# Two transformer blocks on one core: a prologue with its stores and late loads moved behind the first group, one product for the bias lines, an early first slab and a last row in halves

## What is computed

```
mod = silu(c) @ w_ada + b_ada                       # 2048 -> 3 * 2048
shift, scale, gate = split(mod, 3)
h = rmsnorm(x, pre_g) * (1 + scale) + shift
q, k, v, gate_a, u, gate_p = split(h @ w_in)
y_a = windowed_gqa(q, k, v, rel_table, sink) * silu(gate_a)
y_p = multiscale_pool(u, w_pool_grp, pool_scale) * silu(gate_p)
g_a, g_p = split(sigmoid(h @ w_merge + b_merge))
o = (g_a * (y_a @ w_br_attn) + g_p * (y_p @ w_br_pool)) @ w_out
x = x + gate * rmsnorm(o, post_g)
```

## Time and profile before

| | us |
|---|---|
| median of 3 runs (lowest, highest) | 2450.28 (2445.57, 2456.84) |
| profiled execution, its own time | 2450.23 |
| its span | 2448.3 |
| busy in it: PE, DVE, ACT, POOL | 2286.6, 1742.4, 1125.4, 81.2 |
| first product of the main GEMM | 125.45 |

### The profile page before, as it was taken

How to read it: one execution, slowest core, us unless ns; L and a number is a source line. 1 busy time by engine, 2 the same in 40 slices (tenths; PEclk the granted TensorE clock), 3 DMA queues, 4 the chain that set the end, 5 groups by cost and what they waited for, 6 DMA issues and landing times.

```text
span 2448.3 us, 31291 instructions
## 1 busy us (share of the span) xinstructions
PE 2286.6 (93%) x12880; PEld 1973.2 (81%) x12880; DVE 1742.4 (71%) x2015; ACT 1125.4 (46%) x1432; POOL 81.2 (3%) x105
## 2 busy tenths in 40 slices
PE   2499999999998899999999989998999999999998
PEld 1388888888787778888888878787888888888887
DVE  5877867767876677767777788877777777774443
ACT  1243446564445554543455633355444444444443
POOL 1000000001000000000011100000000000000000
PEclk7599999999999999999999999999999999999999
DMA  9967877877883756668876778884555555565552
GB/s 356 411 240 260 287 237 271 295 254 255 307 286 108 274 174 224 228 220 308 277 237 232 254 264 317 312 292 138 189 184 183 185 188 189 189 217 179 173 188 103
DMA packets 245090, 580.56 MB, mean 237 GB/s; under 512 B 11850, under 2 KB 14718, under 8 KB 240596
## 3 DMA queue, kind: packets, MB, share of 16 engines
q1 hardware_dynamic: 232320, 535.86, 63.5%
q0 software_dynamic: 11296, 40.20, 4.7%
q10 hardware_dynamic: 1332, 2.51, 0.3%
HBM read 557.55 MB, written 20.97 MB: 236 GB/s over the span
## 4 chain that ended last, share of the span: by engine, by line
PE 78%; DVE 11%; DMA 7%; ACT 2%; issue 1%; ACTq 0%; DVEq 0%; SPq 0%
PE gemm L1699 46%; PE gemm L1700 23%; DVE w_lo L1059 3%; PE gemm L1703 3%; DMA mod_stage<-in_w_mod 3%; DMA w_stage<-in_w_ada 3%; DVE mod_acc L1053 2%; PE gemm L1702 1%; PE extra L1499 1%; DMA w_stage<-in_w_in 1%; PE extra L1492 1%; ACT w_hi L701 1%; PE extra L1631 1%; DVE mod_acc L1038 1%; PE extra L1607 1%
## 5 line engine op out<-in xcount | busy, mean ns | idle before, releaser
L1699 PE MATMUL gemm<-operand_main,w_hi 128*128 128x512 f32 x4311 | 1560.6, 403 | 49.7 <-DVE operand_main L1110 17.8
L1700 PE MATMUL gemm<-operand_main,w_lo 128*128 128x256 f32 x4311 | 1217.4, 282 | 0.0
L1059 DVE TENSOR_TENSOR w_lo<-w_stage,w_hi 128x1024 fp32r<-128x1024 f32 x736 | 861.2, 1212 | 449.9 <-ACT w_hi L701 449.5
L701 ACT ACTIVATE w_hi<-w_stage 128x1024 fp32r<-128x1024 f32 x736 | 732.2, 1044 | 767.3 <-PE gemm L1700 726.7
L1699 PEld LDWEIGHTS gemm<-operand_main,w_hi 128*128 128x128 f32 x4311 | 820.4, 190 | 241.6 <-issue 28.3
L1700 PEld LDWEIGHTS gemm<-operand_main,w_lo 128*128 128x128 f32 x4311 | 824.4, 191 | 13.5
L1053 DVE SCALAR_TENSOR_TENSOR mod_acc<-mod_stage,c_silu,mod_acc 128x1024 f32<-128x1024 f32 x210 | 267.1, 1301 | 49.3 <-DMA mod_stage<-in_w_mod 43.1
L1699 PE MATMUL gemm<-ffn_hidden,w_hi 128*128 128x512 f32 x688 | 242.9, 397 | 0.0
L1699 PE MATMUL gemm<-operand_attn,w_hi 128*128 128x512 f32 x480 | 180.4, 415 | 15.3 <-DVE proj L1365 10.7
L1700 PE MATMUL gemm<-ffn_hidden,w_lo 128*128 128x256 f32 x688 | 192.5, 280 | 0.0
L1699 PEld LDWEIGHTS gemm<-ffn_hidden,w_hi 128*128 128x128 f32 x688 | 129.1, 188 | 29.5
(11 more groups left out here) (211 smaller groups left out, 1459.3 us busy)
## 6 DMA issues: line engine op xcount, KB each, us to landing
w_stage<-in_w_in SPq DMA_DIRECT2D x128, 1024.0 KB, 6.2
mod_stage<-in_w_mod SPq DMA_DIRECT2D x192, 512.0 KB, 5.9
w_stage<-in_w_up SPq DMA_DIRECT2D x88, 1024.0 KB, 5.0
w_stage<-in_w_down SPq DMA_DIRECT2D x44, 1024.0 KB, 5.0
w_stage<-in_w_ada SPq DMA_DIRECT2D x32, 1024.0 KB, 11.2
w_stage<-in_w_merge SPq DMA_DIRECT2D x32, 1024.0 KB, 5.5
w_stage<-in_w_out SPq DMA_DIRECT2D x32, 1024.0 KB, 7.6
mod_stage<-in_w_ada SPq DMA_DIRECT2D x32, 512.0 KB, 5.7
```

Of the source, the lines that this page charges most:

```text
L701: return nc.scalar.activation(o, i_, f, **kw)
L1059: tt(WL[:, slot_of(n), c0:c1], WST[:, slot_of(n), c0:c1], WH[:, n % HIS, c0:c1].bitcast(F32), ALU.subtract)\
L1699: mm(G[:, m, :], hi, x_of(k), start=(k == 0), stop=False)
L1700: ins = mm(G[:, m, T:2 * T], lo, x_of(k)[:, 0:T], start=False, stop=False)
```

## The change

- The phase order becomes in 0 (without mod rows or pool), u0 (2 rows), u1 (2), in 1 and in 2 (2 each), in 3 (3), in_gates 0 (3) and 1 (2). The pool stages 0 to 3 stand in in 1, in 2, in 3 and in_gates 0.
- Rows use four slots; slab 0 goes into the fifth, loaded ahead of row 4. SP no longer waits for vectors and x. The identity load moves from ACT's to SP's queue. The last row is loaded, added and summed in two halves, into two PSUM banks.
- The first row of each part is a multiplication; GpSimd's two clearing memsets go.
- The vector packs but the first are transposed after the sums of squares. One product with 8 result partitions makes all bias lines, and one store reads them from 8 partitions, 128 times each.
- The x store waits until slab 1 is used (slab_used 2), and with it, in POOL's queue, the line store, w_pool and inv_count.
- split_lo(0) stands between rows 27 and 28, norm_rs(0) and stage_mod_end(0) between rows 24 and 25; splits 1, 2 and 3 stand in the operand loop at steps 7, 12 and 17 (ACT's at tiles 5 and 10 and behind tile 15). scale_half(0) opens the loop, scale_half(1) stands at step 4.

```diff
-        MACC1 = at("mod_acc_scale", [P, D], F32, o_hl)
+        MACC1 = at("mod_acc_scale", [P, D], F32, o_hl + 24 * KB)
...
-        phases.append(Phase("u0", 0, [one(2560)]))
-        phases.append(Phase("u1", 0, [one(3072)], mod=(2, 0, 3)))
-        for n, c in enumerate((0, 512, 1024, 1536)):
-            phases.append(Phase("in", n, [one(c)], mod=(2, 3 + 2 * n, 2), slots=(0, 2),
-                                hooks={0: [("pool_sum", n)], 1: [("pool_mix", n)], 2: [("pool_out", n)]}))
+        pool = lambda n: {0: [("pool_sum", n)], 1: [("pool_mix", n)], 2: [("pool_out", n)]}
+        phases.append(Phase("in", 0, [one(0)]))
+        phases.append(Phase("u0", 0, [one(2560)], mod=(2, 0, 2), slots=(0, 2)))
+        phases.append(Phase("u1", 0, [one(3072)], mod=(2, 2, 2), slots=(0, 2)))
+        for n, c in enumerate((512, 1024, 1536)):
+            phases.append(Phase("in", n + 1, [one(c)], mod=(2, (4, 6, 8)[n], (2, 2, 3)[n]), slots=(0, 2, 1), hooks=pool(n)))
...
-                                post=[("mod_end", 2)] if i else []))
+                                hooks={} if i else pool(3), post=[("mod_end", 2)] if i else []))
...
+            def load_slab(n):
+                ph, g, q = slabs[n]
+                if 0 < n < RAW:
+                    sp.wait_ge(mod0_rows, MOD0_ROWS - ROW_SLOTS + n)
+                elif n:
+                    sp.wait_ge(slab_used, n - RAW + 1)
...
+            sp.dma_start(IDENT[:, :], A["k_ident"]).then_inc(start["ident_in"], 16)
             for t in range(MOD0_ROWS):
                 w, part = mod_w[t // 16]
-                free_slot(t)
-                if t == 4:
-                    sp.wait_ge(start["vec_in"], 16 * sum(len(p) for p in packs[1:]))
-                    sp.wait_ge(start["x_in"], 16)
+                if t == ROW_SLOTS:
+                    load_slab(0)
+                if t >= ROW_SLOTS:
+                    sp.wait_ge(mod0_rows, t - ROW_SLOTS + 1)
...
-            nc.gpsimd.memset(MACC[:, :], 0.0).then_inc(macc_zero, 1)
-            nc.gpsimd.memset(MACC1[:, :], 0.0).then_inc(macc1_zero, 1)
...
+            pool.wait_ge(slab_used, 2)
             pool.wait_ge(xt_copied, 8)
             pool.dma_start(resid.rearrange("t q n -> q t n"), PROJ[:, XT0:XT0 + KT, :]).then_inc(start["x_t_stored"], 16)
-            for h in range(HEADS1):
-                pool.wait_ge(line_copied, h + 1)
-                pool.dma_start(lines[h, 0:P * LINE].rearrange("(q k) -> q k", q=P), LINEB[:, h % 2, :])\
-                    .then_inc(start["lines_stored"], 16)
+            pool.wait_ge(line_copied, 1)
+            pool.dma_start(lines[:, 0:P * LINE].rearrange("h (q k) -> h q k", q=P),
+                           LINE8[:, :].unsqueeze(1).broadcast_to([HEADS1, P, LINE])).then_inc(start["lines_stored"], 16)
...
-                        for first_slab in range(3):
-                            split_hi(first_slab)
+                        for pack in range(1, NP):
+                            copy_vectors(pack)
+                        act.wait_ge(line_mm, 1)
+                        activate(LINE8[:, :], X[0][0:HEADS1, :], ACT.Copy).then_inc(line_copied, 1)
+                        split_hi(0)
...
+                        if k == 0 and t in (5, 10):
+                            split_hi(t // 5)
...
+                    if k == 0:
+                        split_hi(3)
...
+                        if t % 16 == 0:
+                            ins = ts(acc[:, c0:c1], row, CSI[:, 0:1], None, ALU.mult)
+                        else:
+                            ins = stt(acc[:, c0:c1], row, CSI[:, t % 16:t % 16 + 1], acc[:, c0:c1], ALU.mult, ALU.add)
...
+            first_rows(0, 25)
             norm_rs(0)
-            for p in range(2):
-                stage_mod_end(p)
+            stage_mod_end(0)
+            first_rows(25, 28)
+            split_lo(0)
+            first_rows(28, MOD0_ROWS)
+            def scale_half(half):
+                c0, c1 = half * KT // 2, (half + 1) * KT // 2
+                g = col["pre_norm_g"]
+                dve.wait_ge((half_summed, mod_summed)[half], (1, 2)[half])
+                tt(MODV[:, KT + c0:KT + c1], X[2 - half][:, c0:c1], COL[:, mod_b[1] + c0:mod_b[1] + c1], ALU.add)\
+                    .then_inc((half_modv, modv_ready)[half], 1)
+                dve.wait_ge((half_modv, modv_ready)[half], (1, 2)[half])
+                stt(AFF[:, c0:c1], MODV[:, KT + c0:KT + c1], 1.0, COL[:, g + c0:g + c1], ALU.add, ALU.mult)\
+                    .then_inc((half_affine, affine)[half], 1)
...
+                        if k == 0 and s == 4:
+                            scale_half(1)
+                        if k == 0 and s in (7, 12, 17):
+                            split_lo(s // 5)
...
             stage("prep_h", 0, phases[0])
+            for n in range(1, NP):
+                turn_vectors(n)
+            pe.wait_ge(vec_copied, NP)
+            pe.wait_ge(start["line_in"], 32)
+            mm(X[0][0:HEADS1, :], TABX[:, :], OHOT[:, :], start=True, stop=True).then_inc(line_mm, 1)
+            pe.wait_ge(start["const_in"], 32)
             mod_end(0)
-            mod_end(1)
+            for half in range(2):
+                pe.wait_ge((half_row, mod0_rows)[half], (1, MOD0_ROWS)[half])
+                for t in range(8 * half, 8 * half + 8):
+                    ins = mm(X[2 - half][:, t:t + 1], MACC1[:, t * P:(t + 1) * P], ONES[:, 0:1], start=True, stop=True)
+                ins.then_inc((half_summed, mod_summed)[half], 1)
```

More of the change, by code:

```diff
@@ L327, in build @@
                 merged_from.append(ph.slab0 + 2)
-        by_tile_phases = [ph for ph in phases if ph.name in ("u0", "kv2", "up") and ph.i == 0]
+        by_tile_phases = [ph for ph in phases if ph.name in ("in", "kv2", "up") and ph.i == 0]
         named = lambda name: [ph for ph in phases if ph.name == name]
@@ L525, in load_mod_row @@
                         .then_inc(m_landed[half], 16)
-            for n in range(LEAD):
+            for n in range(1, LEAD):
                 load_slab(n)
@@ L647, in _ @@
                 if ph.name == "merge":
-                    pool.wait_ge(start["lines_stored"], 16 * HEADS1)
+                    pool.wait_ge(start["lines_stored"], 16)
                     positive(pool, biased, i)
@@ L701, in activate @@
                 return nc.scalar.activation(o, i_, f, **kw)
-            act.dma_start(IDENT[:, :], A["k_ident"]).then_inc(start["ident_in"], 16)
             for n, pack in enumerate(packs):
@@ L708, in _, with copy_vectors @@
                     act.dma_start(XTOK[:, :, :], A["x"][0].rearrange("(b q) n -> q b n", q=P)).then_inc(start["x_in"], 16)
-            for n in range(NP):
+            def copy_vectors(n):
                 c0 = sum(pack_rows[:n])
@@ L721, in _ @@
                          ACT.Copy).then_inc(xt_copied, 1)
-            act.wait_ge(start["line_in"], 32)
-            for h in range(HEADS1):
-                positive(act, line_mm, h)
-                activate(TABB[:, :], TABX[:, h:h + 1].broadcast_to([33, P]), ACT.Copy).then_inc(line_col, 1)
-                act.wait_ge(line_mm, h + 1)
-                if h >= 2:
-                    act.wait_ge(start["lines_stored"], 16 * h)
-                activate(LINEB[:, h % 2, :], X[h % 2][:, :], ACT.Copy).then_inc(line_copied, 1)
             def split_hi(n):
@@ L1092, in stage @@
                     shift = (0, 3, 6)[k] * KT
-                    if k < 2:
-                        affine_of(k)
-                    for ahead in range(2 if k else 0, 3):
-                        split_lo(ph.slab0 + ahead)
-                    if k:
+                    if k == 0:
+                        scale_half(0)
+                    else:
+                        if k == 1:
+                            affine_of(k)
+                        split_lo(ph.slab0 + 2)
                         norm_rs(norm_of[("prep_h", k)])
-                    dve.wait_ge(affine, k + 1)
+                        dve.wait_ge(affine, k + 1)
                     for s in range(KT + 2):
-                        if s == 11:
+                        if k == 0 and s == 4:
+                            scale_half(1)
+                        if k == 0 and s in (7, 12, 17):
+                            split_lo(s // 5)
+                        if k and s == 11:
                             split_lo(ph.slab0 + 3)
@@ L1218, in hook @@
                         dve.wait_ge(start["pool_in"], 32)
-                        wait_evac(dve, phases[1].groups[0])
+                        wait_evac(dve, first("u1").groups[0])
                     src = PROJ[:, 20 + 2 * k:22 + 2 * k, :]
@@ L1438, in _, with turn_vectors @@
             pe.wait_ge(start["ident_in"], 16)
-            for n in range(NP):
+            def turn_vectors(n):
                 if n:
@@ L1458, in _ @@
                 ins.then_inc(xt_bank, 1)
-            pe.wait_ge(start["const_in"], 32)
             pe.wait_ge(const_set, 2)
-            pe.wait_ge(xt_copied, 8)
-            for h in range(HEADS1):
```

(11 more changed lines are left out.)

73 lines of the change are left out of this document (38 added, 35 removed).

## The result

The changed kernel took 2470.01 us (median of 10 runs, 2459.64 to 2474.13) where the kernel before took 2450.05 (10 runs beside it): a ratio of 1.0074, 95% interval 1.0057 to 1.0091. It is slower by 20 us. I had said 2437, with a range of 2428 to 2449, and so missed both the range and the sign.

The account below looks back on a forecast made before the run. PE was busy 93%, the time to win lying mainly in the DMA-streamed prologue: 20.6 us gained, less 4 (mixed phases), 1 (clock) and 2.5 (moved transfers), gives 13.1, so 2437 from 2450.2; range 2428 to 2449.

Parts of the forecast that it names:

- What moves onto the full stretch: Behind the first group: x store, lines and pool loads moved there cost 2.5 us, bounds 0 and 12.
- a bound of 79: Line store: 79 us for 2.1 MB if it ran at each partition's share of the full rate, 26.5 GB/s.
- rival (a): Behind the first group: line store takes 40 us, slabs come late, PE loses 7, time 2444; chance 0.25.
- the sign's turn at 50 to 55: Line store: the change turns slower where slabs cost 16 us, at a store of some 50 to 55 us.
- Rival (d): Behind the first group: line store takes 79 us, slabs get 53 GB/s, PE stands some 37 us, about 2472; chance 0.08.
- The rule that I had set against the change: Line store: four neighbouring partitions share one port of about 27 GB/s, so an estimated 39 us.
- Gained to the second group: Prologue and first group: the second group starts at 128.9 instead of 149.5, 20.6 us gained.
- The first group's length with its splits inside: First group: with splits 1 to 3 in the operand loop it takes 25.7 us instead of 24.05.
- The 2 to 3 us at the end of in 3: Phase in 3: three mod rows meet a pool stage on DVE, so PE stands 2 to 3 us.
- The x store as hidden work: Start of u0: DVE's wait for the x store costed at nothing; uncovered it would be up to 6 us.
- in_gates 0 should have lost 1.4 to 2.5: Phase in_gates 0: three mod rows and a pool stage together on DVE make PE stand 1.4 to 2.5 us.

Follow-up runs that it names:

- e3: Changed kernel with two copies of each line, the line store reading 16 neighbouring partitions 64 times each; 2451.72 us, ratio 0.9997.
- e1: Changed kernel with the table widened to 16 equal columns per head, the line store reading 128 partitions 8 times each; 2441.7 us, ratio 0.996.
- e5: e1 with mod rows dealt 2 in u0, 3 in u1, 2 each in in 1 to 3, 2 and 3 in in_gates; 2437.19 us, ratio 0.9957.
- e10: Changed kernel with the line store from 128 partitions, issued in the prologue, and mod rows dealt as in e5; 2434.27 us, ratio 0.9924.
- e9: Kernel before with one product and one line store in the prologue, reading 128 partitions 8 times each; 2451.24 us, ratio 0.9996.
- e4: Kernel before with one product and one line store in the prologue, reading 8 neighbouring partitions; 2474.34 us, ratio 1.0088.

## Why the prediction was wrong

**The step that failed** is "What moves onto the full stretch", the 2.5 us (0 to 12) that I took "nearer to the free end since shares leave room". The store's own landing was the open cost; I had written a bound of 79, the 40 of rival (a) and the sign's turn at 50 to 55, and still chose by the DMA share of the stretch it was moved to. Measured: a landing of 51.8 us, 30.4 of waits in u0 and u1, and 6.4 more of clock.

Rival (a) had the store itself nearly right: 40 us, measured 41.9 from the x store's landing, and a pace of the slabs' queue of 105 GB/s, measured 92 to 98. It had wrong what PE still has in hand. It let PE run until 57 us behind the operand loop's start, with slab 7 in place and the slow stretch beginning at slab 8. PE stopped at 44 (149.5), at slab 7: its load was issued at 126.97, behind the line store, and landed at 155.96. Then the low halves of this slab stand behind both halves of a mod row on DVE: from ACT's start of the slab (155.96) to DVE's (168.64) 12.7 us passed, where ACT itself needs about 1 for half a slab. With no row ahead PE would have begun at an estimated 159.4 (DVE began slab 8 1.1 behind ACT, and its two halves take 2.35). So of the 21.5 about 10 are the slab's lateness and about 11.6 the row queued ahead of it. I had counted when slabs come, from one too late on, and not what is queued ahead of them on the engine that splits them.

Rival (d), which I gave 0.08, had the sign, and its 2472 lies near the 2470 by luck: it needs a store of 79 us at 53 GB/s, and neither was there. The sign turns earlier than its 50 to 55: e3, with a landing of 30.8, takes as long as before. The rule that I had set against the change pointed the right way (39 us estimated by it for the store); I gave it a sentence and the sum nothing.

**The prologue, a size.** Gained to the second group: 16.6, said 20.6. Rows began at 13.60 (said 14.4), row 4 started at 27.55 in place of landing at 25.2, the first half of the last row ended at 101.2 (said 97.5), and the operand loop started at 105.29 (said 101.4). The rows are 2.49 apart where nothing is late (the ten from 32.88, the next at 57.74), as said, but there were further waits of about 1.2 and 1.5 at 60.2 and 64.1, and from 25 to 100 us the stream ran at 399 GB/s where I took 424 (the earlier trace rows have 418 and 419). The timeline of the rows:

```profile
13.60 1.28 DVE L1044 TENSOR_SCALAR mod_acc<-w_stage,c_silu 128x2048 f32<-128x2048 f32 x1
...
27.55 2.35 DVE L1046 SCALAR_TENSOR_TENSOR mod_acc<-w_stage,c_silu,mod_acc 128x2048 f32<-128x2048 f32 x1 [3.94 <-DMA w_stage<-in_w_ada]
...
32.88 24.72 DVE L1046 SCALAR_TENSOR_TENSOR mod_acc<-w_stage,c_silu,mod_acc 128x2048 f32<-128x2048 f32 x10 [0.18 <-DMA w_stage<-in_w_ada]
```

The first product came 2.8 behind the loop's start and not 1.8: PE does its 32 column sums in one piece until 108.27, and the second half's sixteen stand ahead of the product in its order. I had let the loop run beside them without asking what PE does first. With this the first product is 4.9 us later than said (108.12 for 103.2), and the first group 0.9 shorter: 4 us.

**Right.** The first group's length with its splits inside (25.7 said; 24.8 from the first product to 132.9). The 2 to 3 us at the end of in 3 (3.09). The x store as hidden work: it landed in 11.1, and no wait of DVE for it shows. **Half right:** in_gates 0 should have lost 1.4 to 2.5 and lost nothing in the changed kernel; in e1, where no late row comes ahead of it, it stood 1.89. e5 shows that both come from rows and pool work in one phase.

**Open.** Behind the start of mod part 2's sums the changed kernel needs 2125.2 us, the kernel before 2134.0, e10 2133.1, e9 2134.9, e4 2135.4, the others 2128.5 to 2133.5, though nothing that I know of differs there. The difference lies in PE's busy time: the same 11673 products take 2049.0 us in the changed kernel and 2056.6 before, at granted clocks of 0.98 and 0.97. Each is one execution, and single times of one kernel lie up to 14 us apart (2459.64 to 2474.13), so I can't tell an effect from scatter; that the profiled execution is 6 below its kernel's median fits scatter. What each of the two parts of the prologue (hold removed, last row halved) gave was not tried alone, and the split of PE's 21.5 into slab and row is an estimate that no run tested.

## What to carry to other kernels

When instructions are saved by giving a transfer a narrower source, price the transfer by which partitions it reads; copies in one product cost nothing here, 128 source partitions in place of 8 neighbours gave 28 us. When the only bounds of a moved cost lie on both sides of the sign, measure or assume the dear one; a DMA share below 1 tells nothing of how a slow transfer holds the others. Count a landing from the landing of what lies ahead in the same queue. And look at what is queued in front of the work that a late transfer feeds: the wait is set by the latest in the line, here half a mod row, 12 us behind the slab. When kernels run on different chips, compare their ratios to a kernel run beside each.

## What I had not expected of the hardware

The store of 2 MB from 8 neighbouring partitions landed in 51.8 us beside slabs and in 62.4 beside the stream of rows, 41.9 and 43.8 of them after the x store ahead of it in the queue had landed; from 16 neighbours 30.8, from 8 partitions four apart 26.0, from all 128 18.0, or 20.6, 15.3 and 8.2 in the second way. While it ran, slabs in packets of about 2.4 KB got 92 GB/s, rows in packets of 7.3 KB 212. All traffic of the changed kernel was at 71 to 95 GB/s from 145 to 162. The engines' share stood at 0.97 for the 22 us from 123, at 73% of e1's bytes.
